# Local attention in a four-layer trunk: rotary rows exchanged by transfers that Pool issues, scores in an area of their own, probabilities scaled and turned in halves

## The chip, the core and the metric

The kernel runs on one NeuronCore of a Trainium2 chip. TensorE (PE in the profile) multiplies matrices into PSUM; VectorE (DVE), ScalarE (ACT) and GpSimd (Pool) work on what is there or in SBUF, each from its own instruction queue; SP issues the weight transfers. Engines are ordered by semaphores alone. The metric is the device time of one execution in microseconds.

## What is computed

A trunk of four layers on 512 tokens of width 1024. Each layer is a token mixer (latent attention, a gated recurrence, local attention, latent attention again) and a squared-ReLU MLP, with a norm before each. The change touches the local attention alone:

```python
def _swa(h, positions, w_in, b_in, sinks, w_o, b_o):          # 16 query heads, 4 key heads of 64
    qkv = h @ w_in + b_in
    q, k, v = jnp.split(qkv, [...], axis=-1)
    q = _rope(q.reshape(B, S, 16, 64), positions, 16)         # the first 16 of 64 rows of a head
    k = _rope(k.reshape(B, S, 4, 64), positions, 16)
    ...                                                       # each 64-token chunk sees itself and the one before
    s = jnp.einsum('bcqhgd,bckhd->bchgqk', q, kw) * 64 ** -0.5
    p = softmax(concatenate([s, sink]))[..., :-1]             # a learned sink for each head
    o = jnp.einsum('bchgqk,bckhd->bcqhgd', p, vw)
    return o @ w_o + b_o

def _rope(x, positions, rot_dim):                             # half = 8
    rot = concatenate([x1 * cos - x2 * sin, x2 * cos + x1 * sin])
```

The rotation needs, beside each row of a head, its partner eight rows away: rows 0 to 7 with rows 8 to 15.

## The kernel before

Activations lie transposed, features on the 128 partitions and the 512 tokens along the free dimension. Weights arrive in units of 512 KB in four slots; for each unit ScalarE writes a rounded part (`w_hi`, L1955) and VectorE the rest (`w_lo`, L1223), a step that both programs call `split`, and TensorE forms each product from three matmuls (L533 to L535). PSUM is cut into four areas of two banks, 0 to 3. An area is claimed by TensorE (`claim(a)`) and freed by whoever reads it last (`area_free[a]`); a fifth such counter, 4, stands for bank 1 of area 3. The order of every engine is written out by hand.

The local attention (`swa`, in four places, one for each engine) first multiplies four units into keys (area 0) and values (area 1). Then there are eight queries, one of 128 rows, two heads, for each i from 0 to 7: `query(i)` is 24 matmuls into bank 0 of an area of `query_area` (3, 1, then 0 and 1 in turn). VectorE scales it into SBUF (`rows_in`, L1773), ScalarE adds the bias (`query_bias`, L2382), TensorE exchanges the partner rows by a product with a permutation, `swap_query`, into bank 1 of the same area (L679), and VectorE multiplies that by the sine (`rotate_swapped`, L1779, which frees the area) and the rest by the cosine and adds (`rotate_rest`, L1784 and L1785). The keys go the same way once, as two such products in area 0 (`swap_keys`), and are then copied for each key head by VectorE (L1807) and ScalarE (L2410).

Attention pass i: `scores(i)` writes 32 small matmuls into area 2 (L1070). VectorE finds the largest (`largest`, L1832 to L1837), ScalarE takes eight exponentials with their sums (`exponentials`, L2388 and L2392) from area 2 and frees it, VectorE divides the whole 128x1024 (`normalised`, L1843 to L1846), TensorE turns the eight blocks (`transposes`, L1086) into area 2 again, VectorE copies one bank of them to SBUF (L1866), ScalarE the other (L2425), `weighted(i)` multiplies by the values (L1100), and ScalarE and VectorE write the head's two parts (`out_hi`, L2400; `head_lo`, L1398). On TensorE pass i runs scores(i), weighted(i-1), query(i+3), transposes(i), swap_query(i+2), for i from 0 to 4. Passes 5 to 7 have pieces of the output product instead of queries (`out(k)`, 12 matmuls each, or half of it). On VectorE a pass is rotate_swapped(i+1), largest(i), rotate_rest(i+1), head_lo(i-1), normalised(i), rows_in(i+3), split, copy of the turned bank 0; on ScalarE it is out_hi(i-1), exponentials(i), split, query_bias(i+3), copy of bank 1. Pool does nothing in the layer between the sums of squares of the norms (L2476); the tables of angles (from L2503) are made in the MLP before it.

## Time and profile before

| | |
|---|---|
| Median of 3 runs | 2122.86 us (2122.58 to 2123.12) |
| The profiled execution | 2122.82 us, span 2121.0 us |
| TensorE busy | 2080.4 us, 98% of the span |
| VectorE, ScalarE, Pool busy | 1162.4, 815.6, 165.9 us |
| Chain that ended last | TensorE 89%, VectorE 6%, ScalarE 4% |
| Issue to landing of a 512 KB weight unit | 3.4 to 4.3 us in the median |

In the profile a line such as L1070 is one of the kernel's; where a helper issues all (the three matmuls of a product, the permutation at L679), its line stands for every caller. Busy time of TensorE is modelled at the ends, and a fixed share of it overlaps from one matmul to the next, so that positions in time are read from starts. The chain that ended last is followed back from the last instruction to what released each; what stands on it is what sets the end.

### The profile page before, as it was taken

Reading aid. Unit: us, or ns where it says so; the run is one execution under the profiler, and the core shown is the slowest. Engines: PE = TensorE matmul, PEld = TensorE weight load, DVE = VectorE, ACT = ScalarE, POOL = GpSimd, SP = SyncE. Lnnn points to the kernel's source line nnn. Section 1 sums busy time; section 2 is a strip of 40 time slices with the busy share of each in tenths; the row PEclk is TensorE's granted clock in tenths of the full one; section 3 lists DMA queues with packets and bytes.
Section 4 is the critical chain, followed back from the end, with each engine's and each line's share of the span. In section 5 each row is a group of like instructions: output and inputs, shape, how many; then the busy total and the mean of one; then the engine's idle time right before and its main releaser. Section 6 shows DMA issues by size and latency. Waiting matters only on the chain.

```text
span 2121.0 us, 25062 instructions
## 1 busy us (share of the span) xinstructions
PE 2080.4 (98%) x9818; PEld 1702.9 (80%) x9818; DVE 1162.4 (55%) x1368; ACT 815.6 (38%) x1156; POOL 165.9 (8%) x184
## 2 busy tenths in 40 slices
PE   8999999999999999999999999999999999999997
PEld 7778888888877888888877788888887778888886
DVE  6766544443886744344667654444476656444344
ACT  6554322323465423132445432232345544232231
POOL 6001000000200200004100100000320001000000
PEclk9999999999999999999999999999999999999998
DMA  6012332233322232323321233223331123223321
GB/s 184 29 60 70 110 99 93 95 99 100 109 70 90 92 98 99 99 90 100 92 80 51 70 110 99 91 97 100 100 94 32 50 80 100 91 97 99 99 90 40
DMA packets 119280, 188.00 MB, mean 89 GB/s; under 512 B 14880, under 2 KB 34208, under 8 KB 119200
## 3 DMA queue, kind: packets, MB, share of 16 engines
q1 hardware_dynamic: 116784, 185.78, 27.3%
q10 hardware_dynamic: 2416, 1.12, 0.2%
q8 instruction: 54, 0.88, 0.2%
q14 instruction: 26, 0.21, 0.0%
HBM read 184.78 MB, written 2.10 MB: 88 GB/s over the span
## 4 chain that ended last, share of the span: by engine, by line
PE 89%; DVE 6%; ACT 4%; issue 1%; DMA 0%; DVEq 0%; SPq 0%; ACTq 0%
PE psum L533 28%; PE psum L534 28%; PE psum L535 28%; ACT arena L2162 1%; PE psum L839 1%; PE psum L826 1%; DVE w_lo L1223 1%; PE psum L953 1%; DVE arena L1532 1%; PE psum L679 1%; DVE small L1518 1%; PE psum L1070 0%; ACT w_hi L1955 0%; PE psum L1100 0%; ACT arena L2150 0%
## 5 line engine op out<-in xcount | busy, mean ns | idle before, releaser
L1223 DVE TENSOR_TENSOR w_lo<-w_raw,w_hi 128x1024 fp32r<-128x1024 f32 x343 | 424.9, 1245 | 794.8 <-ACT w_hi L1955 794.2
L1955 ACT ACTIVATE w_hi<-w_raw 128x1024 fp32r<-128x1024 f32 x343 | 362.6, 1062 | 964.3 <-PE psum L535 964.3
L533 PE MATMUL psum<-h_hi,w_hi 128*128 128x512 f32 x1384 | 546.8, 395 | 0.0
L535 PE MATMUL psum<-h_hi,w_lo 128*128 128x512 f32 x1384 | 538.8, 389 | 0.0
L534 PE MATMUL psum<-h_lo,w_hi 128*128 128x512 f32 x1384 | 538.7, 389 | 0.0
L533 PE MATMUL psum<-u_hi,w_hi 128*128 128x512 f32 x1320 | 519.8, 394 | 6.2 <-DVE w_lo L1223 3.5
L534 PE MATMUL psum<-u_lo,w_hi 128*128 128x512 f32 x1320 | 514.9, 390 | 0.0
L535 PE MATMUL psum<-u_hi,w_lo 128*128 128x512 f32 x1320 | 514.9, 390 | 0.0
L533 PEld LDWEIGHTS psum<-h_hi,w_hi 128*128 128x128 f32 x1384 | 259.9, 188 | 57.5 <-issue 4.3
L534 PEld LDWEIGHTS psum<-h_lo,w_hi 128*128 128x128 f32 x1384 | 259.9, 188 | 56.9 <-issue 4.1
L535 PEld LDWEIGHTS psum<-h_hi,w_lo 128*128 128x128 f32 x1384 | 259.8, 188 | 54.0
L533 PEld LDWEIGHTS psum<-u_hi,w_hi 128*128 128x128 f32 x1320 | 248.6, 188 | 60.4 <-issue 6.9
L534 PEld LDWEIGHTS psum<-u_lo,w_hi 128*128 128x128 f32 x1320 | 248.6, 188 | 52.1 <-issue 1.4
L535 PEld LDWEIGHTS psum<-u_hi,w_lo 128*128 128x128 f32 x1320 | 248.5, 188 | 51.8
L2476 POOL TENSOR_TENSOR ssq<-ssq,sq 128x512 f32<-128x512 f32 x52 | 82.0, 1577 | 1357.1 <-ACT sq L1992 1354.7
L1241 DVE SCALAR_TENSOR_TENSOR h_lo<-x,cols_sb,h_hi 128x512 fp32r<-128x512 f32 x62 | 85.7, 1434 | 3.8 <-ACT h_hi L1968 3.7
L1325 DVE TENSOR_TENSOR arena<-psum,rstd 128x1024 f32<-128x1024 f32 x64 | 78.0, 1219 | 13.8 <-PE psum L535 13.8
L2026 ACT ACTIVATE u_hi<-arena 128x1024 fp32r<-128x1024 f32 x64 | 68.0, 1063 | 34.8 <-DVE arena L1308 32.6
L1328 DVE TENSOR_TENSOR x<-x,arena 128x1024 f32<-128x1024 f32 x64 | 78.4, 1226 | 2.2
L1308 DVE TENSOR_TENSOR arena<-arena 128x1024 f32<-128x1024 f32 x64 | 76.0, 1229 | 0.0
L1312 DVE TENSOR_TENSOR u_lo<-arena,u_hi 128x1024 fp32r<-128x1024 f32 x64 | 76.0, 1228 | 0.0
L1968 ACT ACTIVATE h_hi<-x,cols_sb 128x512 fp32r<-128x512 f32 x64 | 42.9, 717 | 57.2 <-DVE x L1367 24.9
(246 smaller groups left out, 1408.2 us busy)
## 6 DMA issues: line engine op xcount, KB each, us to landing
w_raw<-in_mlp_w SPq DMA_DIRECT2D x256, 512.0 KB, 3.7
w_raw<-in_mla_w_o SPq DMA_DIRECT2D x16, 512.0 KB, 3.5
w_raw<-in_lru_w_in SPq DMA_DIRECT2D x16, 512.0 KB, 4.3
w_raw<-in_swa_w_in SPq DMA_DIRECT2D x12, 512.0 KB, 3.7
w_raw<-in_mla_w_ukv SPq DMA_DIRECT2D x8, 512.0 KB, 4.0
w_raw<-in_lru_w_out SPq DMA_DIRECT2D x8, 512.0 KB, 3.4
w_raw<-in_swa_w_o SPq DMA_DIRECT2D x8, 512.0 KB, 3.6
w_raw<-in_mla_w_in SPq DMA_DIRECT2D x7, 512.0 KB, 3.8
```

The lines of the kernel that those rows point to most:

```text
L533: nc.tensor.matmul(out, stat[0], mov[0], start=start, stop=False, skip_group_check=skip)
L534: nc.tensor.matmul(out, stat[0], mov[1], start=False, stop=False, skip_group_check=skip)
L535: return nc.tensor.matmul(out, stat[1], mov[0], start=False, stop=stop, skip_group_check=skip)
L1223: nc.vector.tensor_tensor(w_lo[:, to], w_raw[:, to], exact(w_hi[:, to]), ALU.subtract).then_inc(w_ready, 1)
L1241: nc.vector.scalar_tensor_tensor(out=LO[k], in0=chunk(x, k), scalar=col(*gain(k)), in1=exact(HI[k]), op0=ALU.mult, op1=ALU.subtract).then_ ...
L1308: nc.vector.tensor_tensor(r, r, r, ALU.mult).then_inc(squared, 1)
L1312: nc.vector.tensor_tensor(chunk(u_lo, 2 * (a + q), 2), chunk(mlp_m["relu"], 2 * q, 2), exact(chunk(u_hi, 2 * (a + q), 2)), ALU.subtract).t ...
L1325: free(nc.vector.tensor_tensor(two(chunk(mlp_m["scaled"], 2 * q, 2)), two(area(a)), twice(rstd2[:, :]), ALU.mult), a)
L1328: nc.vector.tensor_tensor(chunk(x, 2 * a, 2), chunk(x, 2 * a, 2), chunk(mlp_m["scaled"], 2 * q, 2), ALU.add).then_inc(x_ready, 1)
L1955: nc.scalar.activation(w_hi[:, to], w_raw[:, to], ACT.Copy).then_inc(w_hi_done, 1)
L2026: nc.scalar.activation(chunk(u_hi, 2 * (a + q), 2), chunk(mlp_m["relu"], 2 * q, 2), ACT.Copy).then_inc(u_hi_done, 1)
L2476: g.tensor_tensor(to, to, source, ALU.add).then_inc(squares_added, 1)
```

## The change

Four edits, all within the local attention.

1. The partner rows are exchanged by transfers from SBUF to SBUF that Pool issues, four for each 128 rows (two heads, two directions), into `rot` for the queries and into the second half of `p` for the keys. Pool clears both once, so that rows outside the rotation are zero. `swap_keys`, `swap_query` and their products are gone; `rotate` on VectorE waits for the transfers. VectorE's split ahead of the key copies moves ahead of the keys' rotation.
2. Queries 2 to 7 all use area 0, query 1 area 2. Scores of passes 0 to 4 go to area 1, those of 5 to 7 to area 2 as before; the turned probabilities stay in area 2. The products of out(0) into area 1 are made ahead of scores(5).
3. The division, the turning and the waits between them work on halves of four blocks (512 columns).
4. ScalarE copies both turned banks, and adds the bias of query i+3 after them; VectorE's copy is gone.

```diff
+        swa_k_sw = swa_m["p"][:, W_ATT:2 * W_ATT]
+        QUERY_AREA = [3, 2] + 6 * [0]
+        SCORES_AREA = 5 * [1] + 3 * [2]
...
                 def scores(i):
...
-                    claim(2)
-                    pe.wait_ge(area_free[3], c.at("area3"))
+                    to = SCORES_AREA[i]
+                    claim(to)
...
                 def transposes(i):
-                    c.add("p")
-                    pe.wait_ge(p_ready, c.now("p"))
...
-                    claim(2)
-                    claim(3)
-                    for k in range(2 * QB):
-                        mm = nc.tensor.transpose(area(2)[:, k * P:(k + 1) * P], p[:, k * P:(k + 1) * P], ident)
-                    mm.then_inc(psum_done, 1)
+                    for half in range(2):
+                        c.add("p")
+                        pe.wait_ge(p_ready, c.now("p"))
+                        if half == 0:
+                            claim(2)
+                        for k in range(half * QB, (half + 1) * QB):
+                            mm = nc.tensor.transpose(area(2)[:, k * P:(k + 1) * P], p[:, k * P:(k + 1) * P], ident)
+                        mm.then_inc(psum_done, 1)
...
                 query(0)
-                swap_keys()
                 query(1)
-                swap_query(0)
                 query(2)
-                swap_query(1)
                 for i in range(5):
                     scores(i)
                     if i:
                         weighted(i - 1)
                     query(i + 3)
                     transposes(i)
-                    swap_query(i + 2)
-                swap_query(KC - 1)
+                out(0, (2, 3))
                 scores(5)
                 weighted(4)
-                out(0)
+                out(0, (0, 1))
                 out(1)
...
+                def rotate(i):
+                    q, swapped = chunk(m["q"], i), chunk(m["rot"], i % 2)
+                    dve.wait_ge(swa_q_swapped[i % 2], 64 * (i // 2 + 1))
+                    nc.vector.tensor_tensor(swapped, swapped, sin[:, :], ALU.mult)
+                    link(nc.vector.tensor_tensor(q, q, cos[:, :], ALU.mult))
+                    nc.vector.tensor_tensor(q, q, swapped, ALU.add).then_inc(mixed, 1)
+                def rotate_keys():
+                    dve.wait_ge(swa_k_swapped, 64)
...
+                split(1)
                 dve.wait_ge(area_free[3], tables)
-                done("swap keys")
-                rotate(kraw, area(0), 0, scratch, wide=True)
-                nc.vector.tensor_tensor(kraw, kraw, scratch, ALU.add).then_inc(k_rotated, 1)
-                split(1)
+                rotate_keys()
...
                 for i in range(KC):
-                    if i <= 5:
-                        rotate_swapped(i + 1)
-                    if i == 5:
-                        rotate_swapped(7)
                     largest(i)
-                    if i <= 5:
-                        rotate_rest(i + 1)
-                    if i == 5:
-                        rotate_rest(7)
+                    if i < KC - 1:
+                        rotate(i + 1)
                     if i >= 1:
                         head_lo(UHI[i - 1], ULO[i - 1])
-                    normalised(i)
+                    normalised(i, 0)
+                    normalised(i, 1)
                     if i + 3 < KC:
                         rows_in(i + 3)
                     split(1)
-                    done("transposes", i)
-                    nc.vector.tensor_copy(m["pt"][:, 0:T], bank(2, 0)).then_inc(area_free[2], 1)
...
                     split(1)
+                    for half in range(2):
+                        done("transposes", i, half)
+                        ins = nc.scalar.activation(m["pt"][:, half * T:(half + 1) * T], bank(2, half), ACT.Copy)
+                    ins.then_inc(area_free[2], 1)
                     if i + 3 < KC:
                         query_bias(i + 3)
-                    done("transposes", i)
-                    nc.scalar.activation(m["pt"][:, T:2 * T], bank(2, 1), ACT.Copy).then_inc(area_free[3], 1)
...
+                if kind == "swa":
+                    g.memset(swa_k_sw, 0.0)
+                    g.memset(swa_m["rot"], 0.0).then_inc(swa_cleared, 1)
+                    pool.wait_ge(swa_cleared, 1)
+                    def swap_rows(to, rows, swapped):
+                        for at in (0, SW_D):
+                            for a, b in ((at, at + 8), (at + 8, at)):
+                                g.dma_start(to[a:a + 8, :], rows[b:b + 8, :]).then_inc(swapped, 16)
+                    pool.wait_ge(biased, 2)
+                    swap_rows(swa_k_sw, swa_m["p"][:, 0:W_ATT], swa_k_swapped)
+                    for k in range(KC):
+                        pool.wait_ge(biased, 2 + k + 1)
+                        if k >= 2:
+                            pool.wait_ge(mixed, 1 + k - 1)
+                        swap_rows(chunk(swa_m["rot"], k % 2), chunk(swa_m["q"], k), swa_q_swapped[k % 2])
```

## Rows read from the trace of the kernel before

**Rows 1.** Stretches: length, busy PE, PEld, DVE, ACT, POOL; clock, DMA share, GB/s
```profile
1080.18:1100.01 19.83, 19.83 (x82) 14.68 (x80) 15.97 (x24) 9.14 (x13) 0.00 (x0) 1.00 0.22 71
1100.01:1110.22 10.21, 8.74 (x67) 6.44 (x67) 7.74 (x14) 7.14 (x22) 0.00 (x0) 1.00 0.05 19
1110.22:1152.05 41.83, 39.95 (x394) 30.19 (x395) 33.11 (x57) 23.04 (x84) 0.00 (x0) 1.00 0.15 52
1152.05:1185.48 33.43, 30.60 (x333) 24.43 (x332) 21.36 (x37) 16.84 (x62) 0.00 (x0) 1.00 0.20 64
```

**Rows 2.** Chain that ended last, one pass: start us, us, engine, tile, line
```profile
1131.06 1.10 PE psum L1070 x28
1132.16 1.08 PE psum L1100 x32
1133.24 0.43 PE psum L533
...
1138.68 0.24 PE psum L535
...
1138.94 0.69 DVE arena L1773
1139.64 1.13 DVE w_lo L1223
1140.77 0.61 DVE arena L1866
...
1141.47 1.10 PE psum L1070 x29
```

**Rows 3.** The same chain at the end of the fifth pass
```profile
1149.33 1.07 PE psum L1086 x8
1150.40 1.72 PE psum L679 x4
```

**Rows 4.** Timeline of PE: start us, us, line, form, count, idle before
```profile
1100.01 1.10 PE L1070 MATMUL psum<-arena 64*64 64x64 f32 x32
...
1110.22 1.10 PE L1070 MATMUL psum<-arena 64*64 64x64 f32 x32 [0.43 <-DVE arena L1866]
...
1185.48 0.50 PE L533 MATMUL psum<-u_hi,w_hi 128*128 128x512 f32 x1 [1.42 <-DVE u_lo L1398]
```

**Rows 5.** Timeline of DVE, key copies and one pass
```profile
1092.17 1.72 DVE L1807 COPY arena<-arena 64x512 f32<-64x512 f32 x4
...
1132.28 0.17 DVE L1832 MEMSET psum<- 64x128 f32 x1 [0.72 <-PE psum L1070]
...
1134.02 0.68 DVE L1784 TENSOR_TENSOR arena<-arena,cos 128x512 f32<-128x512 f32 x1
...
1137.17 0.17 DVE L1843 TENSOR_TENSOR small<-small 128x8 f32<-128x8 f32 x1 [1.14 <-ACT arena L2392]
...
1137.61 1.23 DVE L1846 TENSOR_TENSOR arena<-arena,small 128x1024 f32<-128x1024 f32 x1
```

**Rows 6.** Timeline of ACT: key bias, weight split, key copies
```profile
1082.94 1.34 ACT L2377 ACTIVATE arena<-arena,cols_sb 128x512 f32<-128x512 f32 x2 [3.22 <-DVE arena L1789]
...
1087.07 1.04 ACT L1955 ACTIVATE w_hi<-w_raw 128x1024 fp32r<-128x1024 f32 x1
1091.15 2.56 ACT L2410 ACTIVATE arena<-arena 64x512 f32<-64x512 f32 x4 [3.04 <-DVE arena L1803]
```

**Rows 7.** DMA issues of 16 KB, us to landing; ACT queue issuing four
```profile
arena<-in_positions SPq DMA_DIRECT2D x8, 16.0 KB, 2.7
...
arena<-in_positions ACTq DMA_DIRECT2D x4, 16.0 KB, 3.7
...
1.18 1.87 ACTq L419 DMA_DIRECT2D arena<-in_positions  x4
```

**Rows 8.** Costly groups on POOL, forms apart: busy us, mean ns, idle before
```profile
L2476 POOL TENSOR_TENSOR ssq<-ssq,sq 128x512 f32<-128x512 f32 x52 | 82.0, 1577 | 1357.1 <-ACT sq L1992 1354.7
...
L2503 POOL CAST arena<-arena 128x128 f32<-128x128 int32 x3 | 3.3, 1098 | 527.4 <-DMA arena<-in_positions 527.4
```

More of the change, by code:

```diff
@@ L362, in trunk @@
         mixed = sem("mixed")
-        rows_scaled = sem("rows_scaled")
+        half_exp_done = sem("half_exp_done")
+        swa_cleared = sem("swa_cleared")
+        swa_k_swapped = sem("swa_k_swapped")
+        swa_q_swapped = [sem(f"swa_q_swapped{i}") for i in range(2)]
         k_rotated = sem("k_rotated")
@@ L1028, in swa @@
                 outs_before = c.now("area4")
-                query_area = [3, 1] + [i % 2 for i in range(2, KC)]
                 def query(i):
                     next_unit_ready()
-                    a = query_area[i]
+                    a = QUERY_AREA[i]
                     claim(a)
+                    jobs["swa", "query area", i] = c.now(f"area{a}")
                     wh, wl = unit()
@@ L1041, in query @@
                     used("query", i)
-                def swap_query(i):
-                    pe.wait_ge(biased, 2 + i + 1)
-                    swap_rows(bank(query_area[i], 1), 1, chunk(swa_m["q"], i)).then_inc(psum_done, 1)
-                    summed("swap", i)
-                def swap_keys():
-                    pe.wait_ge(biased, 2)
-                    claim(0)
-                    for b in range(2):
-                        mm = swap_rows(bank(0, b), 1, chunk(swa_m["p"], b))
-                    mm.then_inc(psum_done, 1)
-                    summed("swap keys")
                 def scores(i):
@@ L1060, in scores @@
                     pe.wait_ge(mixed, 1 + i + 1)
-                    claim(2)
-                    pe.wait_ge(area_free[3], c.at("area3"))
-                    jobs["swa", "scores area", i] = c.now("area2")
+                    to = SCORES_AREA[i]
+                    claim(to)
+                    jobs["swa", "scores area", i] = c.now(f"area{to}")
                     for b in range(QB):
@@ L1077, in transposes @@
                 def transposes(i):
-                    c.add("p")
-                    pe.wait_ge(p_ready, c.now("p"))
                     p = swa_m["p"][:, (i % 2) * W_ATT:(i % 2 + 1) * W_ATT]
-                    claim(2)
-                    claim(3)
-                    jobs["swa", "turned areas", i] = c.now("area2"), c.now("area3")
-                    for k in range(2 * QB):
-                        mm = nc.tensor.transpose(area(2)[:, k * P:(k + 1) * P], p[:, k * P:(k + 1) * P], ident)
-                    mm.then_inc(psum_done, 1)
-                    summed("transposes", i)
+                    for half in range(2):
[6 more added lines that the diff above has]
+                        mm.then_inc(psum_done, 1)
+                        summed("transposes", i, half)
+                    jobs["swa", "turned area", i] = c.now("area2")
                 def weighted(i):
-                    for a, n in zip((2, 3), jobs["swa", "turned areas", i]):
-                        pe.wait_ge(area_free[a], n)
+                    pe.wait_ge(area_free[2], jobs["swa", "turned area", i])
                     claim(4)
@@ L1106, in out @@
                 def out(k, ms=range(4)):
-                    if k % 2 == 0 and ms[0] == 0:
+                    if k == 0 and 2 in ms:
+                        jobs["swa", "before out"] = {name: c.now(name) for name in ("tensor_unit", "area0", "area1")}
+                        claim(1)
+                    if k == 0 and 0 in ms:
+                        claim(0)
+                    if k % 2 == 0:
                         next_unit_ready()
-                    if k == 0:
-                        jobs["swa", "before out"] = {name: c.now(name) for name in ("tensor_unit", "area0", "area1")}
-                        claim(0)
-                        claim(1)
                     pe.wait_ge(area_free[4], outs_before + k + 1)
@@ L1761, in swa @@
                 split(1)
-                query_area = [3, 1] + [i % 2 for i in range(2, KC)]
                 def done(*name):
@@ L1810, in swa @@
                 rows_in(1)
-                rotate_swapped(0)
-                rotate_rest(0)
+                rotate(0)
                 split(1)
@@ L1830, in largest @@
                     done("scores", i)
+                    a = SCORES_AREA[i]
                     nm, sp = eights(nmax, i), eights(sink_part, i)
-                    link(nc.vector.memset(two(area(2))[0:CHUNK, :, 0:CHUNK], NEG))
-                    link(nc.vector.tensor_reduce(nm, area(2).rearrange("p (k n) -> p k n", n=P), AX.X, ALU.max,
+                    link(nc.vector.memset(two(area(a))[0:CHUNK, :, 0:CHUNK], NEG))
+                    link(nc.vector.tensor_reduce(nm, area(a).rearrange("p (k n) -> p k n", n=P), AX.X, ALU.max,
                                                  negate=True))
@@ L2379, in query_bias @@
                 def query_bias(i):
-                    act.wait_ge(rows_scaled, i + 1)
+                    act.wait_ge(area_free[QUERY_AREA[i]], jobs["swa", "query area", i])
                     t = chunk(m["q"], i)
```

41 lines of the change are left out of this document (22 added, 19 removed).

## The prediction

> **What bounds the kernel now.** I read the stretches first, then the chain that ended last, then TensorE's own timeline, and last what VectorE and ScalarE do in one pass. The diff touches only the local attention layer, so the ledger runs from the start of query(0) at 1080.18 us to the start of out(7) at 1185.48, 105.30 us. The stretches [rows 1] show TensorE with no idle time before the first scores, 1.47 us idle in the first pass, 1.88 us in the next four and 2.83 us in the tail, at the full granted clock throughout. It is the bound, and VectorE, at 33.11 of 41.83 us, is the only other candidate. The chain of one pass [rows 2] shows where its idle time sits: scores 1.10, weighted 1.08, a query of 5.68 (1133.24 to 1138.92), and then not TensorE but VectorE: the scaled query 0.69, the weight split 1.13, the copy of the turned probabilities 0.61, and 0.12 us between pieces, 10.41 us in all. TensorE does transposes and a swap beside these and waits for the copy at the end, since the next scores need the area that the copy frees. The fifth pass ends in two swaps and no wait [rows 3]: transposes 1.07, two swaps 1.72.
>
> **The change, part by part.** I write S_i for the start of scores(i).
>
> *Swaps leave TensorE.* Two take 1.72 us [rows 3], so one takes 0.86. Eight query swaps and two key halves are removed: 10 x 0.86 = 8.6 us of TensorE. In the loop 0.86 of it lies beside VectorE's copy.
>
> *The loop.* scores(i+1) now write area 1, free since the exponentials of pass i. What stays behind a query is the transposes: 1.10 + 1.08 + 5.68 + 1.07 = 8.93 us a pass; the measured fifth pass gives the same, 10.65 (1141.47 to 1152.12) less 1.72 [rows 2, 3]. Against 10.41 this is 1.48 us less, three times from S_1 to S_4. Is VectorE quick enough? Its pass from the memset: largest 1.74 (1132.28 to 1134.02), rotation 0.61 + 0.72 + 0.61, head_lo 0.61, two halves of (0.44 + 0.61) instead of 0.44 + 1.23, rows_in 0.61, split 1.13: 8.2 us [rows 2, 5]. Halving adds 0.43 and the removed copy gives 0.61 back. Counted from S_i: memset at 1.22, largest done 2.96, rotation 4.90, head_lo 5.5, half 0 at 6.55, half 1 at 7.6. TensorE reaches the transposes at 7.86, so both halves are there. rows_in ends at 8.7, split at 9.85, and the next memset is due at 8.93 + 1.22 = 10.15. Cover: 0.3 us. Gone, each 0.1 us past it costs 0.1 a pass.
>
> *Both copies on ScalarE.* I price each at 0.67, half of its two 128x512 biases [rows 6]. Counted from S_i, half 0 is turned at 8.4 and copied to 9.1, half 1 turned at 8.93 and copied to 9.8. Who waits is weighted(i), and scores(i+1) stand ahead of it until 8.93 + 1.10 = 10.03: cost nothing, with 0.2 us of cover; each 0.1 past it costs 0.1 a pass. Behind the two waits on ScalarE stands the bias of query i+3, done at 10.5; it feeds a transfer with slack (below).
>
> *Transfers Pool issues.* Nine swaps of four transfers, 36 in all. No row shows Pool issuing one. Write g for Pool's time per transfer and L for issue to landing; a swap takes X = 3g + L. For g: four transfers of the same 16 KB take ScalarE's queue 1.87 us, 0.47 each [rows 7]; a Pool operation takes up to 1.58 us, and a 1.10 us one stands at the head of each table of angles [rows 8]. I take 1.1: the transfers' own instructions may be as slow as the cold operation, and the 0.47 is another engine's. For L: 2.7 and 3.7 us for 16 KB [rows 7]; I take 2.7, these being eight of the twelve. X = 6.0, bounds 4.1 (0.47, 2.7) and 8.5 (1.58, 3.7). Below nothing is excluded, since a transfer can't give time back. What queues behind Pool's waits is the other swaps only; Pool does nothing else in all four stretches [rows 1]. Its two memsets of 128x1024, at most 6.3 us at 1.58 for each 128x512 [rows 8], stand ahead of the first stretch and hide there. SP's queue is not touched.
> The Trainium skill, page "DMA: Bandwidth & Descriptors", section "Anatomy of one DMA", gives about 2.0 us plus bytes / 436 GB/s for a transfer issued by GpSimd; with an estimate of 2.04 in place of 2.7 X would be 5.3 and the sum 1.4 us less. No row here shows it.
>
> *The start, where X is on the path.* Key bias ends at 1084.28 [rows 6], so swapped keys are there at r = 1084.5 + X = 1090.5. (Not before 1089.3: the split moved ahead of them waits for ScalarE's, 1087.07 to 1088.1 [rows 6], and takes 1.13.) In the kernel before TensorE swapped them and they cost no wait. From r: three wide operations 3.6 (1.23 each, a little overlapped), four copies 1.72 [rows 5], rows_in(1) 0.6, rotation of query 0 2.0, a hand-over 0.1: S_0 = r + 8.05 = 1098.55. TensorE is done with three queries at 1100.01 less 4 x 0.86 = 1096.6, so 2.0 of the 3.4 us freed go into a wait. Then ScalarE: key copies, 2.56 [rows 6], to r + 6.2, bias(1) to r + 6.9; swap 1 lands at r + 7.0 + X = r + 13.0. VectorE meanwhile: split, rows_in(2) to r + 9.8, largest to r + 11.55. It waits 1.5 us for swap 1; rotation to 15.05, halves 16.1 and 17.15. TensorE waits too: query(3) now needs the area of query(2), free at r + 9.8, ends at r + 15.6; the second half of the transposes runs 17.25 to 17.8. S_1 = r + 17.8 = 1108.3, against 1110.22: 1.9 us less [rows 4]. All other swaps have slack: bias(i+3) is done 1.6 us after S_(i+1), its rotation comes 2.96 after S_(i+2), which leaves 10.3 us for X = 6.0, and Pool needs 4g = 4.4 of each 8.93.
>
> *The tail.* S_4 = 1108.3 + 3 x 8.93 = 1135.1. S_5 = S_4 + 8.93 + 1.4 (six matmuls of out(0) put ahead, 6 x 0.23) = 1145.4. S_5 to S_6: 1.10 + 1.08 + 18 x 0.23 brings TensorE to 6.4, but half 1 is ready at 7.6: transposes end at 8.3, two products of out(2) 1.4: 9.75. S_6 to S_7: 24 matmuls instead, 10.3, no wait. S_7 to out(7): no rotation, exponentials whole at 6.11 [rows 5], half 1 at 7.15, transposes to 7.75, out(6) 9.2, weighted 10.3, then ScalarE's and VectorE's halves of the head 1.4: 11.7. So out(7) starts at 1145.4 + 31.75 = 1177.2, against 1185.48 [rows 4].
>
> **Sum.** 1.9 at S_1, 3 x 1.48 = 4.5, 0.3 at S_5 with out(0) half done, 1.6 in the tail: 8.3 us. After out(7) the two programs do the same. The profiled execution took 2122.82 us (span 2121.0), the median is 2122.86. 2122.8 - 8.3 = 2114.5.
>
> **The rivals.**
> (a) Cheap transfers, X near 4.1. r falls to 1089.3 and S_1 = r + 16.8 = 1106.1, as VectorE no longer waits for swap 1: 2.2 us more, 2112.3. For: the queue's 0.47. Against: that row is another engine's.
> (b) Dear transfers that stay in step, g from 1.6 to 2.4. Past X = 5 both the keys and swap 1 move with X, so each us of X costs 2: X = 8.5 gives 2119.5, X = 10 gives 2122.5.
> (c) Slower: Pool becomes the bound. With 4g over 8.93 it never catches up; the last of 36 transfers lands at 1084.4 + 35g + 2.7, its rotation takes 2.0, then 11.7 to out(7). Equal to before at g = 2.4; g = 3 gives 1205.8, or 2143. For: nothing here shows that Pool issues one in less. Against: its whole 128x512 operations take 1.58 [rows 8].
> (d) VectorE becomes the bound of the loop: the 0.3 us of cover goes if a two-input operation of SBUF is slowed by Pool beside it or a wait costs 0.2 more. At 9.5 us a pass 4 to 5 passes lose 2.5: 2117.
> (e) The issue waits for VectorE. If Pool can write only while VectorE is idle, 21% of the loop [rows 1], g = 1.1 / 0.21 = 5.2 and (c) gives 1084.4 + 182 + 2.7 + 13.7 = 1283, or 2220. The Trainium skill, page "SBUF — State Buffer", section "Who interferes with whom", speaks of such a lock: descriptor generation is shut out while a VectorE copy in a two-port mode runs, but not by a two-input tensor_tensor. By that rule only the four key copies, 1.72 us, could do it. They run at r + 3.65, 1094.2, after swap 0 was issued (1084.4 + 8.8 = 1093.2) and before swap 1, so the rule gives nothing.
>
> **How the numbers follow.** Forecast 0.55, (a) 0.15, (b) 0.12, (c) 0.07, (d) 0.08, (e) 0.03. The range goes from 2110.5, below (a) for a landing under 2.7, to 2122, the end of (b); that leaves out a little of (a) and (b), (c) and (e), under 0.2. About 0.2%, 4.2 us, is what a measurement of this kernel can tell from no change. Forecast, (a) and most of (d) are faster by more: 0.74; most of (b) is the same, with a little of (d): 0.16; slower 0.10.
>
> **What would show each step.** S_0 near 1098.5 with a wait of 2 us ahead of it; S_1 near 1108.3 with VectorE's rotation waiting for a transfer; S_2, S_3, S_4 8.9 us apart and nothing idle ahead of scores; the transposes of pass 5 in two pieces 0.6 us apart; out(7) near 1177. Pool's rows give g, the landing of its transfers L. It would be wrong if X is over 8, if the passes are 9.5 us apart, or if TensorE's granted clock falls after the wait at S_0; before, waits of 1.4 us left it whole.

## The result and the profile after

| | before | after |
|---|---|---|
| median of the runs timed together, us | 2122.72 (4 runs) | 2109.88 (4 runs) |
| ratio, 95% interval | | 0.994 (0.9928 to 0.9952) |
| the profiled execution, us | 2122.82 | 2109.62 |
| start of query(0) to start of out(7), us | 105.30 | 93.52 |
| the rest of the profiled execution, us | 2017.5 | 2016.1 |

The change is faster by 12.8 us in the medians, and by 13.2 us in the profiled executions. 11.8 of these lie in the attention layer and 1.4 ahead of it. Forecast were 2114.5 and a range from 2110.5: the sign was right, the size too small, and the time lies 0.6 us outside the range.

The positions are those of the prediction, S_i for the start of scores(i). Query(0) starts at 1080.18 us before and at 1078.82 after, so a position of after is compared with the forecast once 1.36 is added to it.

| us | S_0 less query(0) | S_0 to S_1 | S_1 to S_4 | S_4 to S_5 | S_5 to S_6 | S_6 to S_7 | S_7 to out(7) | sum |
|---|---|---|---|---|---|---|---|---|
| before | 19.83 | 10.21 | 31.25 | 10.58 | 10.35 | 10.25 | 12.83 | 105.30 |
| forecast | 18.37 | 9.75 | 26.79 | 10.33 | 9.75 | 10.3 | 11.7 | 97.0 |
| after | 17.25 | 8.65 | 26.03 | 10.09 | 9.62 | 10.06 | 11.82 | 93.52 |

The stretches of after, in the columns of [rows 1]: to the first scores, the first pass, the next four, the tail.

```profile
1078.82:1096.07 17.25, 16.38 (x74) 13.22 (x72) 14.35 (x23) 9.11 (x12) 5.19 (x10) 1.00 0.27 73
1096.07:1104.72 8.65, 7.83 (x65) 6.21 (x65) 7.88 (x17) 6.56 (x21) 3.22 (x7) 1.00 0.27 78
1104.72:1140.80 36.08, 36.08 (x391) 29.95 (x390) 32.79 (x65) 26.19 (x90) 8.19 (x16) 1.00 0.22 67
1140.80:1172.30 31.50, 29.32 (x327) 23.42 (x326) 20.69 (x43) 18.43 (x66) 2.06 (x4) 1.00 0.23 71
```

In the third row TensorE is busy for the whole stretch, where [rows 1] showed 1.88 us idle. VectorE is at 32.79 of 36.08 us, 91%, where it was at 79%. Pool now appears, with its 2.05 us of issuing per swap.

The chain that ended last, for one pass (start us, us, engine, tile, line), to be laid beside [rows 2]:

```profile
1104.79 1.03 PE psum L1063 x26
1105.82 1.08 PE psum L1093 x32
1106.90 0.43 PE psum L540
...
1112.34 0.23 PE psum L542
1112.57 0.87 PE psum L1079 x8
1113.44 0.58 PE psum L1063 x11
```

Scores 1.03, weighted 1.08, a query of 5.67, transposes 0.87: 8.65 us. No VectorE line is left between the query and the next scores, where [rows 2] had three, 2.43 us together.

What still interrupts TensorE stands in brackets in its timeline (start us, us, line, tile, form, count, idle before): at the first scores, ahead of query(3), which waits for the area of query(2) as the forecast had it, at the last transposes, and ahead of out(7). The transposes of the sixth pass wait 0.36 us in the same way between their two halves.

```profile
1096.07 1.10 PE L1063 MATMUL psum<-arena 64*64 64x64 f32 x32 [0.87 <-issue]
1097.86 0.47 PE L540 MATMUL psum<-h_hi,w_hi 128*128 128x512 f32 x1 [0.68 <-DVE arena L1761]
...
1167.79 0.66 PE L1079 MATMUL psum<-const_sb,arena 128*128 128x128 f32 x4 [0.34 <-DVE arena L1840]
...
1172.34 0.50 PE L540 MATMUL psum<-u_hi,w_hi 128*128 128x512 f32 x1 [1.42 <-DVE u_lo L1388]
```

Now the transfers, which no row of before showed. Pool's timeline has four of a swap grouped in one row; the first row is the keys, the last the swap of query 1.

```profile
1083.56 2.27 POOL L2546 DMA_DIRECT2D arena<-arena  x4 [20.80 <-ACT arena L2364]
...
1095.19 2.05 POOL L2546 DMA_DIRECT2D arena<-arena  x4 [7.04 <-ACT arena L2369]
```

Four take 2.05 us, so g, Pool's time per transfer, is 0.51; only the very first took more, 0.73. The DMA issues, with KB each and the median us to landing:

```profile
arena<-arena POOLq DMA_DIRECT2D x32, 16.0 KB, 2.4
arena<-arena POOLq DMA_DIRECT2D x4, 32.0 KB, 2.1
```

In its timeline VectorE starts the keys' rotation (first row) with no wait for their transfers, straight behind its weight split. It waits for a transfer once in the layer, for the swap of query 1:

```profile
1087.95 1.22 DVE L1775 TENSOR_TENSOR arena<-arena,sin 128x1024 f32<-128x1024 f32 x1
...
1100.03 0.69 DVE L1768 TENSOR_TENSOR arena<-arena,sin 128x512 f32<-128x512 f32 x1 [0.48 <-DMA arena<-arena]
```

From the first issue at 1095.19 to VectorE's start at 1100.03 are 4.84 us: this is X, the time of a whole swap as the forecast defined it, at the one place where somebody waits for it. Less three issues, 1.53, its landing took 3.3, longer than the median of 2.4. The chain that ended last shows what the wait does: into S_1 it runs over VectorE's division of the second half, which the wait has made late.

```profile
1103.38 0.70 DVE arena L1840
...
1104.13 0.66 PE psum L1079 x4
```

The wait belongs to this execution and not to the kernel. In the repeat a1 (below), the same kernel, the four transfers of this swap landed after 1.8 us each, X was 3.3, and VectorE did not wait; its first pass took 8.49 us for 8.65. Single landings scatter from 1.8 to 3.7 us in the profiled execution of after.

The Trainium skill, page "DMA: Bandwidth & Descriptors", section "Anatomy of one DMA", gives about 2.0 us plus the bytes over the rate for a transfer that GpSimd issues. The keys' median of 2.1 agrees with it. The median of 2.4 of the queries and the waited-for landing of 3.3 are longer, and the measurement decides.

Last, the 1.4 us outside the layer. In the recurrence TensorE waits 3.47 us before and 3.46 us after for the same weight split, and runs at the lower of its two clock levels, 1.2 GHz, for a while behind it. The stretches 668 to 676 and 676 to 684 us, before and then after, in the columns of [rows 1]:

```profile
668.00:676.00 8.00, 4.53 (x17) 3.40 (x16) 6.84 (x7) 3.90 (x4) 0.00 (x0) 0.84 0.11 30
676.00:684.00 8.00, 8.00 (x28) 6.38 (x27) 1.47 (x3) 1.06 (x1) 0.00 (x0) 0.74 0.67 234
```

```profile
668.00:676.00 8.00, 4.54 (x17) 3.41 (x16) 6.84 (x7) 3.90 (x4) 0.00 (x0) 0.86 0.10 30
676.00:684.00 8.00, 8.00 (x34) 6.55 (x33) 2.59 (x3) 1.06 (x1) 0.00 (x0) 0.93 0.67 235
```

With the granted clock at 0.74 TensorE gets 28 matmuls into 8 us, at 0.93 it gets 34. The change doesn't touch this stage, so whether the six matmuls belong to the change had to be asked of more runs.

### The profile page after: what moved, and what is told of

Its sections match the earlier page's. It is cut to its first block, busy times and chain, and to the rows that moved or that the text cites. A ratio compares the mean times of both kernels' runs of the same rounds, so it can differ in the third digit from the quotient of the medians.

```text
span 2107.8 us, 25097 instructions
## 1 busy us (share of the span) xinstructions
PE 2069.8 (98%) x9798; PEld 1698.9 (81%) x9798; DVE 1158.0 (55%) x1384; ACT 819.3 (39%) x1164; POOL 186.8 (9%) x222
## 4 chain that ended last, share of the span: by engine, by line
PE 89%; DVE 6%; ACT 4%; issue 1%; DMA 0%; POOL 0%; DVEq 0%; SPq 0%; ACTq 0%
PE psum L540 28%; PE psum L542 28%; PE psum L541 28%; ACT arena L2149 1%; PE psum L846 1%; PE psum L833 1%; DVE w_lo L1213 1%; PE psum L960 1%; DVE arena L1522 1%; DVE small L1508 1%; ACT w_hi L1942 0%; PE psum L1063 0%; PE psum L686 0%; PE psum L1093 0%; PE psum L1079 0%
```

## The experiments

All kernels compute the whole layer. Unless something else is said, an edit is on the changed kernel. The ledger is the time from query(0) to out(7).

| kernel | median us | ratio to before, 95% interval | ledger |
|---|---|---|---|
| e2, eight transfers a swap | 2113.04 (5 runs) | 0.9959 (0.9945 to 0.9974) | 97.22 |
| e1, swaps on TensorE | 2118.80 (10 runs) | 0.9984 (0.9974 to 0.9993) | 101.86 |
| e3, transfers alone | 2131.04 (5 runs) | 1.0040 (1.0025 to 1.0054) | 113.61 |
| e5, transfers alone, late rotation | 2122.13 (10 runs) | 1.0000 (0.9990 to 1.0009) | 105.18 |
| e4, scores in area 2 | 2114.22 (5 runs) | 0.9960 (0.9946 to 0.9974) | 96.83 |
| e6, whole division | 2113.04 (4 runs) | 0.9957 (0.9942 to 0.9972) | 96.90 |
| e7, a copy on VectorE | 2113.16 (4 runs) | 0.9956 (0.9941 to 0.9972) | 96.66 |
| a1, the changed kernel again | 2109.98 (5 runs) | 0.9941 (0.9928 to 0.9955) | 93.38 |
| b3, start only | 2109.97 (5 runs) | 0.9942 (0.9929 to 0.9956) | 92.63 |
| b2, tail only | 2108.38 (5 runs) | 0.9936 (0.9922 to 0.9950) | not comparable |
| b1, start and tail | 2108.09 (5 runs) | 0.9934 (0.9920 to 0.9947) | not comparable |

The kernel before had medians of 2122.21 beside e1 to e4 (16 runs), 2122.25 beside e5 to e7 and b1 (15), and 2122.39 beside a1, b2 and b3 (9). In b1 and b2 matmuls of another group stand ahead of out(7), so that their ledgers can't be compared. Code is shown in part, with "..." where lines are left out.

### e2: what a longer transfer costs

```diff
...
-                                g.dma_start(to[a:a + 8, :], rows[b:b + 8, :]).then_inc(swapped, 16)
+                                for h in (0, 4):
+                                    g.dma_start(to[a + h:a + h + 4, :], rows[b + h:b + h + 4, :]
+                                                ).then_inc(swapped, 16)
```

> The changed kernel with each swap in eight transfers of four rows and not four of eight. Pool issues one in 0.51 us and it lands 2.4 after, so that X goes from 3 x 0.51 + 2.4 = 3.9 to 7 x 0.51 + 2.4 = 6.0, the value that the prediction had assumed. Theory A (the prediction's own working was right and its price was wrong): S_1 comes 2.2 us later and the passes stay 8.7 apart, ledger 95.7, 2112. Rival H (the transfers are hidden whatever they cost): ledger 93.5. Rival P (Pool at work slows VectorE beside it): the passes grow too, ledger over 97.

Measured: a ledger of 97.22, 3.7 more, where 2.2 more was expected. Pool's timeline (two swaps in one row) and VectorE's waits:

```profile
1096.34 8.17 POOL L2547 DMA_DIRECT2D arena<-arena  x16 [4.78 <-ACT arena L2369]
```

```profile
1089.09 1.23 DVE L1775 TENSOR_TENSOR arena<-arena,sin 128x1024 f32<-128x1024 f32 x1 [1.45 <-DMA arena<-arena]
1103.32 0.69 DVE L1768 TENSOR_TENSOR arena<-arena,sin 128x512 f32<-128x512 f32 x1 [2.62 <-DMA arena<-arena]
```

Sixteen transfers of half the rows in 8.17 us are 0.51 each again: the price is one of the instruction, not of the bytes. Four more issues lengthen X at swap 1 by 2.1 us, to 6.98. The keys, which nobody waited for, are now waited for by 1.45 us, and swap 1 by 2.62 instead of 0.48. S_0 comes 1.5 later and S_0 to S_1 grows by 2.1, together 3.6, while the passes stay at 8.68 to 8.70, which is against rival P, though the ledger lies over its 97. So X counts twice at the start and not at all in the loop, as the prediction had it ("each us of X costs 2"): 3.7 for 2.1 is 1.8 per us. The expectation had taken the median landing, and swap 1's last one took 3.4 us. What was wrong in the prediction was the value put in.

### e1, e3 and e5: the swaps and the rest, each without the other

e1 undoes the transfers alone and keeps the other edits:

```diff
...
                     query(i + 3)
                     transposes(i)
+                    swap_query(i + 2)
+                swap_query(KC - 1)
                 out(0, (2, 3))
...
```

> The changed kernel with its first edit undone: TensorE swaps the partner rows again, ten products of 0.86 us, into bank 1 of the areas; areas, halves and copies stay as changed. I count the ledger from the start of query(0) to the start of out(7): 105.3 us before, 93.5 after. Theory A (a pass is the longer of two loops, TensorE's own work and the loop through VectorE and the shared area; both had to be shortened): the passes become 8.69 + 0.86 = 9.55 us, the 1.9 us of waits at the start go, ledger 93.5 + 8.6 - 1.9 = 100.2, 2116.6. Rival R (the gain is the swaps and nothing else): all of it is lost, ledger 105 and 2121 or more.

Measured: ledger 101.86. Its second to fourth pass are 9.52 us, and the chain of one says why:

```profile
1125.20 0.87 PE psum L1093 x8
1126.07 0.86 PE psum L685 x2
1126.93 1.03 PE psum L1077 x26
```

The swap (L685) stands whole in the chain, 8.66 + 0.86 = 9.52. S_0 stands 19.81 behind query(0), as before. The fifth pass is 12.52 us, 2.43 more than in the changed kernel: 1.72 are its two swaps, and about 0.7 is a cost of my edit, in which the last swap waits (0.49 us idle) for the last bias. The ledger is 1.7 over the 100.2 expected.

e3 puts the transfers into the kernel before and changes nothing else. VectorE's sine multiply, which now waits for a transfer, stays where the kernel before had it, ahead of the row maximum:

```diff
...
                 def rotate_swapped(i):
-                    done("swap", i)
-                    nc.vector.tensor_tensor(chunk(scratch, i % 2), bank(query_area[i], 1), sin[:, :], ALU.mult
-                                            ).then_inc(area_free[query_area[i]], 1)
+                    dve.wait_ge(swa_q_swapped[i % 2], 64 * (i // 2 + 1))
+                    t = chunk(scratch, i % 2)
+                    nc.vector.tensor_tensor(t, t, sin[:, :], ALU.mult)
...
```

> The kernel before with the first edit alone: Pool's transfers in place of the swaps, with the old areas, whole divisions and VectorE's copy. Theory A: the passes stay at 10.4 us, since they are set by query, scaling, split and copy on VectorE, and the swaps were beside the copy; the gain is 2.6 us ahead of S_0 and 1 to 2 us in the fifth pass, ledger 101 to 102, 2119. Rival R: the 8.6 us of the swaps go from the time, ledger 96.7, 2114.

Measured: 2131.04 us, slower than before by 8.8, and a ledger of 113.61. Both theories failed. The third to the fifth pass are 10.42 to 10.46, as theory A said, but the first two are 14.13 and 12.01 and the sixth is 15.13. VectorE's timeline has the reason; TensorE's timeline and the stretch from 1108.33, in the columns of [rows 1], have the consequence:

```profile
1101.00 0.69 DVE L1767 TENSOR_TENSOR arena<-arena,sin 128x512 f32<-128x512 f32 x1 [2.37 <-DMA arena<-arena]
...
1158.14 0.69 DVE L1767 TENSOR_TENSOR arena<-arena,sin 128x512 f32<-128x512 f32 x1 [3.20 <-DMA arena<-arena]
```

```profile
1108.33 1.97 PE L1078 MATMUL psum<-const_sb,arena 128*128 128x128 f32 x8 [4.56 <-DVE arena L1834]
1111.13 1.99 PE L1062 MATMUL psum<-arena 64*64 64x64 f32 x32 [0.83 <-DVE arena L1854]
1113.04 1.86 PE L1092 MATMUL psum<-arena 128*64 128x64 f32 x32
```

```profile
1108.33:1116.00 7.67, 6.84 (x77) 5.89 (x78) 5.60 (x10) 2.36 (x7) 2.05 (x4) 0.59 0.27 79
```

VectorE stands 2.37 us at the transfer in the first pass (3.20 in the sixth, where query 7 is rotated in the same pass as query 6), and behind it in its queue stand the maximum, the exponentials' input and the division that TensorE needs. TensorE waits 4.56 us, and then its granted clock is 0.59 for 7.67 us: transposes take 1.97 for the 1.09 us of e5 (below), scores 1.99 for 1.10, weighted 1.86 for 1.15. A wait of VectorE is thus paid with a wait of TensorE and, here, with its clock.

e5 is e3 with VectorE's rotations moved as the changed kernel moves them: all of them behind the maximum, and that of query 7 from the sixth pass to the seventh:

```diff
                 for i in range(KC):
-                    if i <= 5:
-                        rotate_swapped(i + 1)
-                    if i == 5:
-                        rotate_swapped(7)
                     largest(i)
-                    if i <= 5:
+                    if i < KC - 1:
+                        rotate_swapped(i + 1)
                         rotate_rest(i + 1)
-                    if i == 5:
-                        rotate_rest(7)
...
```

> The transfers of edit 1 on the kernel of before, with VectorE's order of the changed kernel: the sine multiply and sum of pair i+1 stand behind the row maximum of pair i, so that Pool has two passes' worth of VectorE's work between a query and its use. Theory A (what made the transfers alone slower was VectorE standing at a transfer in the first pass and the sixth, ahead of the maximum that TensorE waits for): with the wait moved behind the maximum the first pass is about 11 us, passes 1 to 4 stay at 10.4 (scores, turned blocks and weighted values take turns in one accumulator area), the sixth is 10.4 and the tail 10.3, 10.3 and 12.8 as before; the ledger from query 0 to output group 7 is 17.9 + 11 + 3 x 10.4 + 10.4 + 33.4 = 104, and the time 2121. Theory R (the transfers free TensorE of its swaps, and that alone is worth the sum of 0.86 us each wherever the order allows): ledger 97, time 2114. Theory B (the order of VectorE has nothing to do with it): ledger 113, 2131, as with the transfers alone.

Measured: ledger 105.18 for an expected 104, and a time equal to before. The place of VectorE's sine multiplies is worth 8.9 us (2131.04 less 2122.13, from two batches); how it divides between the two moves no run shows. And 8.6 us less work for TensorE is worth nothing here: the third to the fifth pass stay at 10.42 to 10.45, since they end in VectorE's copy and not in the swap. TensorE's timeline, and a stretch of the first pass:

```profile
1104.91 1.09 PE L1078 MATMUL psum<-const_sb,arena 128*128 128x128 f32 x8 [1.68 <-DVE arena L1834]
...
1107.30 1.99 PE L1062 MATMUL psum<-arena 64*64 64x64 f32 x32 [1.29 <-DVE arena L1849]
...
1119.12 1.10 PE L1062 MATMUL psum<-arena 64*64 64x64 f32 x32 [1.69 <-DVE arena L1849]
```

```profile
1107.30:1112.30 5.00, 5.00 (x71) 4.34 (x72) 2.80 (x6) 1.39 (x7) 1.25 (x3) 0.69 0.37 123
```

Where the swap was, TensorE is now idle for VectorE's copy (L1849), 1.69 us. The start gains 1.9 us at S_0 and loses 2.0 in the first two passes, part of it by the clock, granted at 0.69 from 1107.30 on (scores 1.99 for 1.10).

The ledgers together: transfers alone 0.1 (e5), everything but the transfers 3.4 (e1), both 11.8; VectorE's new order is in all three. 8.2 us (7.5 without what e1 pays for its own edit) belong to neither, but to their meeting. A pass is the longer of two chains, TensorE's own with the swap in it and the one over VectorE's copy; each edit shortens one of them.

### e4, e6 and e7: the other edits, one by one

e4 gives the scores their old area back, after the turned probabilities:

```diff
-        SCORES_AREA = 5 * [1] + 3 * [2]
+        SCORES_AREA = 8 * [2]
```

> The changed kernel with all scores in area 2, where the turned probabilities are. Theory A: scores(i+1) wait until ScalarE has copied both halves, 0.9 us after the transposes end; passes of 9.6 us from S_1 to S_4, the fifth is covered by the pieces of out(0), ledger 93.5 + 3.5 = 97.0, 2113.4. Rival C (the early halves make the copy finish in time, and the area of its own brings nothing): 93.5 and 2109.9.

Measured: ledger 96.83, passes of 9.33 to 9.58, as theory A had it. The hand-over is in the chain again, now over ScalarE's two copies (L2414):

```profile
1122.53 0.45 PE psum L1079 x4
...
1123.00 1.09 ACT arena L2414 x2
1124.10 0.14 issue
1124.23 1.10 PE psum L1063 x28
```

e6 divides in one piece:

```diff
-                    normalised(i, 0)
-                    normalised(i, 1)
+                    normalised(i)
```

> The changed kernel with the division of the probabilities done in one piece after both exponentials; the rest as changed. Theory A (passes 0 to 3 of the loop are bound by TensorE, whose query work stands between scores and turning, so the halves only show where there is no query work: the sixth to the eighth pass): passes 0 to 3 stay at 8.7 to 8.8, the sixth and seventh grow by 0.6 each and the last by about 1.0; ledger 95.5, time 2111.9. Theory R (the halves are what shortens each pass): each of the eight passes 0.6 to 0.7 longer, ledger 98.5 to 99, time 2115.

Measured: ledger 96.90, between the two theories. The halves are worth 0.8 in the first pass, 0.15 to 0.20 in each of the next four, 0.65 and 0.2 in the sixth and seventh, and 1.0 in the last. TensorE's timeline, first, second and sixth pass, and the chain in the second:

```profile
1105.85 1.09 PE L1079 MATMUL psum<-const_sb,arena 128*128 128x128 f32 x8 [0.97 <-DVE arena L1836]
...
1114.71 1.09 PE L1079 MATMUL psum<-const_sb,arena 128*128 128x128 f32 x8
...
1151.55 1.09 PE L1079 MATMUL psum<-const_sb,arena 128*128 128x128 f32 x8 [1.34 <-DVE arena L1836]
```

```profile
1114.72 1.08 PE psum L1079 x8
```

TensorE waits 0.97 in the first pass and 1.34 in the sixth. In between, the division of 1.22 us that VectorE starts at 1113.43 ends 0.15 us after the start of the query's last matmul in the chain (1114.50), and the wait behind it is too short to be shown. The transposes then take 1.08 in the chain, for 0.87 in that of after. Theory A was right that the halves show most where there is no query work, but had forgotten the first pass and took the 0.15 to 0.20 of the others for nothing.

e7 gives VectorE the copy of the first half back:

```diff
                     split(1)
+                    done("transposes", i, 0)
+                    nc.vector.tensor_copy(m["pt"][:, 0:T], bank(2, 0)).then_inc(swa_pt0, 1)
```

> The changed kernel with VectorE copying the first half of the turned probabilities out of the accumulator, as in the kernel before, after its split; ScalarE copies the second half. Theory A (VectorE's chain of rows, split and copy then ends the pass: 32.8 of 36.1 us busy in the loop, and the copy adds 0.7 a pass and sits behind the split): passes 9.3, ledger 96, time 2112.4. Theory R (ScalarE's two copies one behind the other are what ends the pass, and sharing them is no loss): passes 8.4 to 8.7, ledger 92.5 to 93.5, time 2109 to 2110.

Measured: ledger 96.66; the first pass is 8.49, the next three 9.39 to 9.42, the fifth 11.18 for 10.09. The chain of one pass has 0.66 us between scores and weighted, and in VectorE's timeline the copy ends there:

```profile
1125.31 1.03 PE psum L1066 x26
1126.35 0.66 issue
1127.00 1.15 PE psum L1097 x32
```

```profile
1125.08 1.22 DVE L1217 TENSOR_TENSOR w_lo<-w_raw,w_hi 128x1024 fp32r<-128x1024 f32 x1
1126.22 0.68 DVE L1859 COPY arena<-psum 128x512 f32<-128x512 f32 x1
```

Edit by edit, each taken away from the whole, the ledger grows by 8.3 (transfers, 0.7 of it the cost of my edit), 3.3 (area), 3.4 (halves) and 3.1 (copy): 18.1 for a gain of 11.8. The same microseconds are counted more than once, because each edit takes away one of several waits that end at nearly the same time. e7's first pass, 8.49, is no gain of the copy: it equals that of a1 (below), where VectorE does not wait for swap 1 either.

### a1: the 1.4 us outside the layer

The changed kernel once more, unedited.

> The changed kernel once more, nothing edited. The profiled executions of the two kernels differ by 13.2 us, 11.8 of them in the attention layer and 1.4 ahead of it, where TensorE ran a few microseconds at 1.2 GHz behind a wait of 3.5 us in the recurrence. Theory C (how long that low clock lasts changes from execution to execution and is no property of the change): the layer's ledger is 93.5 again within 0.1, and the median of many executions, with the kernel before run alongside, differs by 11.8 +- 0.4: 2110.4. Theory P (the change shortens that stretch too): the difference is 13.2, the time 2109.0.

Measured: ledger 93.38, and 12.4 us between the medians of the two kernels. The stretches of the recurrence this time, in the same columns:

```profile
668.00:676.00 8.00, 4.54 (x19) 3.44 (x18) 6.84 (x7) 3.90 (x4) 0.00 (x0) 0.95 0.05 7
676.00:684.00 8.00, 8.00 (x31) 6.45 (x30) 2.75 (x3) 1.06 (x1) 0.00 (x0) 0.84 0.77 258
```

Over both rows TensorE got 45 matmuls before, 51 after and 50 here. Counted matmul by matmul, 13 of them ran 0.43 us apart instead of 0.23 in the profiled execution of before, 6 in that of after, 8 here; in the ten other kernels from 5 (e4) to 13 (e6). Two executions of the same kernel have 6 and 8; e6, an edit of the changed kernel, has as many as the kernel before, and e3 and e5, edits of the kernel before, have 8 and 6. The count is for theory C. The medians alone decide nothing: 12.4 lies between theory C's 11.8 +- 0.4 and theory P's 13.2. The layer's share is 11.8 to 11.9, and what the medians show beyond it, 12.8 and 12.4, is within the spread of single runs (2107.4 to 2111.8 for the changed kernel in nine). The first pass differs too, 8.49 for 8.65: Pool's row and VectorE's for the swap of query 1 are these, with no wait at the transfer.

```profile
1095.90 2.04 POOL L2546 DMA_DIRECT2D arena<-arena  x4 [7.03 <-ACT arena L2369]
```

```profile
1100.18 0.69 DVE L1768 TENSOR_TENSOR arena<-arena,sin 128x512 f32<-128x512 f32 x1
```

### b1 to b3: the waits that are left

The start: the rows and bias of query 1 ahead of the key copies, one weight split of VectorE taken out of the start and made up for in the sixth pass, the queries in turns in areas 0 and 3. The tail: in the sixth pass the division ahead of the next rotation, and 12 matmuls of output group 2 ahead of out(7).

```diff
-        QUERY_AREA = [3, 2] + 6 * [0]
+        QUERY_AREA = [3, 2, 0, 3, 0, 3, 0, 3]
...
+                square_group((2, 3), UHI, ULO, anything, part=0)
                 out(7)
-                square_group((2, 3), UHI, ULO, anything)
+                square_group((2, 3), UHI, ULO, anything, part=1)
...
```

> The changed kernel with its remaining idle stretches of TensorE attacked: the rows and the bias of query 1 ahead of the key copies, its split behind the first rotation; the queries after it in turns in two accumulator areas; in the sixth pass the division ahead of the next rotation; and the first 12 matmuls of output group 2 ahead of output group 7. Theory A (the idle times are waits that these orders end): the start is 1.0 shorter, the sixth pass 0.6, the wait of 1.4 ahead of output group 7 is filled: ledger 90.5, time 2107. Theory R (the waits are only moved to the next instruction, since VectorE is 91% busy there): ledger 93 to 93.5, time 2109.5. Should the key copies that are moved back be what the first scores wait for, the ledger is 94.5, time 2111.

> The changed kernel with only the orders at the start of the layer changed, as in the run of start and tail together: rows and bias of query 1 ahead of the key copies, its split behind the first rotation, the queries in turns in two accumulator areas. There the first scores came 0.14 earlier and the first pass was 7.88 for 8.65. Theory A (these 0.9 us reach the end, since TensorE has no wait behind them): ledger 92.6, 0.9 below the changed kernel's time of the same batch. Theory R (the wait ahead of output group 7 hangs on VectorE and ScalarE, not on TensorE, and takes them back): ledger 93.5.

> The changed kernel with only the tail changed: the division ahead of the next rotation in the sixth pass, and 12 matmuls of output group 2 ahead of output group 7. Theory A (the wait of 1.4 us is filled by matmuls that are ready): 1.4 us below the changed kernel's time of the same batch, TensorE shows no wait behind the last weighted values. Theory R (the wait moves to the accumulators: the area that output group 2 claims comes free later than its first matmuls ask for it): less than 0.5 us.

Measured: b3's ledger is 92.63, 0.75 less than a1's, but its time equals a1's (2109.97 and 2109.98); its profiled execution had 11 or 12 slow matmuls in the recurrence, that of a1 8. 0.75 us is less than five runs can tell. b2 is 1.60 us below a1 for an expected 1.4, and in TensorE's timeline the last weighted values are followed by matmuls of group 2 with no idle time in brackets. The sixth pass is 9.25 for 9.64. Runs of the two kernels overlap (2108.18 to 2109.08, 2107.89 to 2111.77), so it is the trace that shows the wait gone, and the size is rough. b1, timed apart from these, gave 2108.09, the lowest median of the study; against the changed kernel's 2109.9 that is 1.8, for the 3 expected. Its seventh pass is 10.59 us, 10.05 in b2, which takes back most of what the start gives; only b1 has both the second weight split and the late rotation in its sixth pass. That it is better than b2 isn't shown.

## Why the prediction was right and wrong

**Right: what bounds the pass.** The forecast took the three VectorE pieces of [rows 2] out of the chain, saw that the swap would otherwise take their place, and found no new wait. The stretch from S_1 to S_4 has none, the query lies between scores and transposes as it said, and the cover was there: e4, e6 and e7, each of which takes away one of the things that the cover rests on, lengthen the passes by 0.9, 0.2 and 0.7.

**Mis-sized: the pass.** Forecast 8.93, measured 8.68, three times, 0.76 in all. The scores are 1.03 in the chain of after, where the forecast took the 1.10 of a chain with a wait ahead of them [rows 2]. Its check by the fifth pass missed this: 10.65 ran to the end of a swap, while from start to start the pass is 10.58, and 8.86 less the swaps. The transposes are 0.87, not the 1.07 of [rows 3]. That 1.07 was already a price with a short wait in it, since the whole division ended just then (in the pass of [rows 5] at 1137.61 + 1.23 = 1138.84, 0.16 behind the start of the query's last matmul at 1138.68 [rows 2]). e6, with the whole division back, has 1.08 and passes of 8.85 to 8.87. So 0.2 of the 0.25 is what the halves give in the loop, where the forecast had them give nothing. The fifth pass was too long by 0.24 for the same reasons.

**The step that failed: "Transfers Pool issues".** Between 0.47, another engine's queue [rows 7], and Pool's own operations of 1.10 and 1.58 us [rows 8], I took 1.1 for one issue. It took 0.51, in 35 of the 36 transfers after and at half the bytes in e2. The row of the same kind of work, an issue, on another engine was the better neighbour than the row of the same engine with other work. With the landing of 2.7 this would have given X = 4.2; measured were 4.84 at swap 1, landing 3.3. At the start this is worth 2.2: S_1 was forecast 28.1 after query(0) and came after 25.9. The keys' rotation started 1.2 earlier, at 1087.95 + 1.36 = 1089.31, the 1089.3 that the weight split sets, and VectorE waited 0.48 at swap 1 instead of 1.5. TensorE waited 0.87 ahead of S_0 instead of 2.0, and its granted clock stayed at 1.00 behind that. That is case (a), which had S_1 at 1106.1; measured is 1104.72 + 1.36 = 1106.08. It had 15 in 100. That the two agree to 0.02 is luck: (a) has no wait at swap 1, its X was 4.1, and the X there was 4.84 in one execution and 3.3 in the other, with S_1 0.17 earlier behind query(0).

**Right: the tail, and its halves.** From S_5 to out(7) 31.75 was forecast and 31.50 measured, and e6 shows the halves at work in the sixth, seventh and eighth pass. The two pieces of the transposes of the sixth pass start 1.0 apart and not 0.6.

**Not foreseen: the run of the recurrence.** The prediction set the rest of the program equal. In the two profiled executions it differs by 1.4 us, by the granted clock behind a wait that both have. The forecast was made against a profiled execution of before which happened to have 13 slow matmuls; in the 40 runs timed beside the experiments its medians are 2122.2 to 2122.4, not 2122.8. So the error of 4.9 us in the profiled execution is 2.2 (price of a transfer) + 1.0 (passes) + 0.3 (tail) + 1.4 (clock elsewhere), and the price of a transfer is the largest term. The range was bounded by case (a) less a shorter landing; it held neither the shorter passes nor the clock, and either would have carried it below 2109.9.

**The rivals.** (b) and (c) fall with g = 0.51: Pool is busy 2.05 us of a pass. e2 keeps to (b)'s slope. (d) and (e): with Pool issuing beside them VectorE's operations take 0.69 and 1.23 us, for 0.68 and 1.23 in [rows 5], and Pool's four issues 2.04 to 2.05 us in each pass of the loop, though VectorE is 91% busy. The swap issued at 1095.19 runs for 1.9 of its 2.05 us beside VectorE's two-input operations. The Trainium skill, page "SBUF — State Buffer", section "Who interferes with whom", exempts a two-input tensor_tensor from the lock on descriptor generation, and the trace agrees; the four key copies ran while Pool issued nothing, so no run shows the lock itself.

**What the result rests on beside the four edits.** e3 and e5 show a step that the prediction passed over in one clause: the sine multiply was put behind the maximum. On the kernel before, the transfers without it cost 8.8 us, and with it nothing.

## What to carry to other kernels

Work taken off the bounding engine is worth what the chain beside it allows: 8.6 us of TensorE's swaps gave 0.1 alone and 8.3 on top of the other edits (7.6 without the cost of the edit that put them back), so follow both chains to the point where they meet before pricing either. When a result comes from a transfer, put the instruction that waits for it behind whatever the bounding engine needs from the same queue. A price read from a row that stood beside a wait can have a part of that wait in it. For an operation that the trace doesn't show, take as neighbour the row of the same kind of work on another engine rather than that of other work on the same engine, and let the range hold the scatter of the stages that the change leaves alone.

## What the runs showed of the hardware

- A transfer between two SBUF regions that Pool issues takes it 0.51 us, with 16 KB as with 8 KB, and 2.04 to 2.05 for four with VectorE 91% busy beside it; the first four of a layer, the keys, took 2.27. The landings of the queries' transfers of 16 KB had medians of 2.4 in after and a1, 3.0 in e3 and 2.9 in e5; single ones took from 1.8 us to 3.7 in after and to 4.4 in e3. The one that VectorE waited for took 3.3 in after and 1.8 in a1, the same kernel.
- TensorE's granted clock fell behind a wait of 3.5 us in the recurrence and of 4.56 us in e3 (0.59 over 7.67 us), and scores ran at half speed behind two waits of 1.68 and 1.29 us in e5, which ended at 1104.91 and 1107.30. It stayed at 1.00 behind single waits of 0.5 to 1.4 us in the layer, behind those of 1.5 to 1.7 us ahead of the scores in e5's later passes, and behind one of 2.40 us ahead of the first scores in e2, which took 1.10. How long it stays low differs between executions of one kernel (6 and 8 slow matmuls), by 0.2 us for each matmul at the lower level.
